# Where two roots, one sum of squares and the first sums stand in a fused two-block kernel

## What is computed

```
h = rmsnorm(x, norm_mix[l])                       # first layer: x / sqrt(mean(x*x) + eps) * gain
proj = einsum('btd,de->bte', h, w_in[l])
...
y = ssd_chunked(xh, dt, a, bm, cm) + d_skip[:, None] * xh
y = y.reshape(bsz, seq, D_SSD) * silu(z)
yg = y.reshape(bsz, seq, SSD_GROUPS, D_SSD // SSD_GROUPS)        # two halves of 512 channels
yg = yg * rsqrt(mean(yg * yg, axis=-1, keepdims=True) + EPS)     # a root for each half
y_ssd = yg.reshape(bsz, seq, D_SSD) * norm_w
...
q = rms_norm(q, q_norm_w); k = rms_norm(k, k_norm_w)             # norms by head, next stage
```

## Time and profile before

| what | us |
|---|---|
| median of 3 runs (lowest, highest) | 2328.26 (2328.11, 2329.42) |
| the profiled execution | 2329.49 |
| its span, first to last instruction | 2327.3 |
| PE busy in it | 2270.1 (98%) |
| VectorE busy | 1140.6 (49%) |
| ScalarE busy | 980.1 (42%) |
| GpSimd busy | 980.8 (42%) |
| mean granted clock of PE | 0.993 |

### The profile page before, as it was taken

One profiled execution on the slowest core, in us unless ns is written; L12 is line 12 of the kernel. 1 busy time (PEld: TensorE's weight loads), 2 busy tenths in 40 slices (PEclk: granted clock), 3 DMA queues, 4 the chain that ended last, 5 costly groups with the idle time before them and its releaser, 6 DMA issues.

```text
span 2327.3 us, 29177 instructions
## 1 busy us (share of the span) xinstructions
PE 2270.1 (98%) x10536; PEld 1791.7 (77%) x10560; DVE 1140.6 (49%) x1475; ACT 980.1 (42%) x1489; POOL 980.8 (42%) x453
## 2 busy tenths in 40 slices
PE   7989999999999999999999999999999999999999
PEld 6866678888888876678888887876777667888887
DVE  6866664222334786665222334647776543433300
ACT  5546643222214545644333213335535663534311
POOL 5962234444443982234444443432442113544442
PEclk9999999999999999999999999999999999999999
DMA  4321123333662221123323472322121002332332
GB/s 161 91 63 56 55 82 91 95 95 99 199 210 79 89 75 46 55 73 91 99 90 99 161 240 87 91 82 63 57 86 50 28 28 72 109 93 96 99 93 88
DMA packets 59842, 216.00 MB, mean 93 GB/s; under 512 B 6640, under 2 KB 6896, under 8 KB 59760
## 3 DMA queue, kind: packets, MB, share of 16 engines
q1 hardware_dynamic: 52272, 187.62, 26.4%
q10 hardware_dynamic: 7488, 27.27, 3.5%
HBM read 212.76 MB, written 2.10 MB: 92 GB/s over the span
## 4 chain that ended last, share of the span: by engine, by line
PE 88%; DVE 6%; ACT 3%; issue 2%; DMA 0%; SPq 0%; DVEq 0%; ACTq 0%
PE bank L1305 26%; PE bank L1307 26%; PE bank L1306 26%; PE bank L1770 1%; PE bank L1448 1%; PE bank L1318 1%; PE bank L1774 1%; PE bank L1508 1%; PE bank L1488 1%; PE bank L1379 1%; PE bank L1758 1%; PE bank L1374 1%; ACT prob L497 1%; DVE tmp L1233 1%; DVE tmp L1227 1%
## 5 line engine op out<-in xcount | busy, mean ns | idle before, releaser
L310 POOL TENSOR_TENSOR wl<-raw,wh 128x1024 fp32r<-128x1024 f32 x351 | 855.0, 2437 | 1301.9 <-ACT wh L383 1301.9
L1305 PE MATMUL bank<-hh,wh 128*128 128x512 f32 x2024 | 815.9, 403 | 28.4 <-DMA cst<-consts 11.7
L1307 PE MATMUL bank<-hh,wl 128*128 128x512 f32 x2024 | 793.1, 392 | 0.0
L1306 PE MATMUL bank<-hl,wh 128*128 128x512 f32 x2024 | 792.7, 392 | 0.0
L383 ACT ACTIVATE wh<-raw 128x1024 fp32r<-128x1024 f32 x351 | 369.6, 1053 | 631.8 <-PE bank L1307 580.7
L1305 PEld LDWEIGHTS bank<-hh,wh 128*128 128x128 f32 x2024 | 383.3, 189 | 122.5 <-issue 18.9
L1306 PEld LDWEIGHTS bank<-hl,wh 128*128 128x128 f32 x2024 | 383.4, 189 | 86.6 <-issue 9.6
L1307 PEld LDWEIGHTS bank<-hh,wl 128*128 128x128 f32 x2024 | 382.5, 189 | 81.7
L1305 PE MATMUL bank<-ah,wh 128*128 (+1 forms) x528 | 208.1, 394 | 0.0
L1307 PE MATMUL bank<-ah,wl 128*128 (+1 forms) x528 | 207.0, 392 | 0.0
L1306 PE MATMUL bank<-al,wh 128*128 (+1 forms) x528 | 204.9, 388 | 0.0
(11 more groups left out here) (325 smaller groups left out, 2555.7 us busy)
## 6 DMA issues: line engine op xcount, KB each, us to landing
raw<-stream SPq DMA_DIRECT2D x351, 512.0 KB, 3.6
ada_w<-ada ACTq DMA_DIRECT2D x48, 512.0 KB, 4.6
x<-x_t ACTq DMA_DIRECT2D x4, 512.0 KB, 7.9
out_t<-x SPq DMA_DIRECT2D x8, 256.0 KB, 2.1
cst<-consts SPq DMA_DIRECT2D x1, 640.0 KB, 4.8
tmp<-masks SPq DMA_DIRECT2D x1, 320.0 KB, 5.1
par<-params SPq DMA_DIRECT2D x1, 253.0 KB, 6.1
cst<-consts SPq DMA_DIRECT2D x1, 224.0 KB, 9.6
```

Of the source, the lines that this page charges most:

```text
L310: nc.gpsimd.tensor_tensor(wl[:, slot, :], raw[:, raw_slot, :], wh[:, slot, :].bitcast(F32), ALU.subtract).then_inc(lo_ready, 1)
L1305: mm(dst, wh[:, slot, w], xh, start=start, stop=False)
L1306: mm(dst, wh[:, slot, w], xl, start=False, stop=False)
L1307: return mm(dst, wl[:, slot, w], xh, start=False, stop=stop)
```

## The change

It moves work and adds none.

- ScalarE, pair loop: the root of the first half goes from turn 5 to behind the last turn, directly ahead of the second half's root. The copy of v tile 5, which stood ahead of that root, is again taken in turn 6 like the others.
- VectorE: the first half's reciprocal and its four products go from turns 5, 6 and 7 to behind the loop; there each half now has a reciprocal and four products, one half behind the other.
- ScalarE, q tiles: the eight copies of normed y go from ahead of the q tiles to behind the rounding of a chunk in the first of them, ahead of that tile's square.
- PE, q tiles: the last sum of squares of y and the last turn of v go from ahead of kk 6 of q tile 0 to ahead of kk 0 of q tile 1.
- PE, start of the first layer: the wait for the constants goes from ahead of the first matmul to ahead of `sum_both_ways`, and that goes from behind the two first tiles to ahead of kk 7 of the first tile. The second layer keeps its order.

```
@@ scalar, pair loop
             for t in range(1, KT):
                 exp_within(t)
-                if t != 6:
-                    copy_v(t - 1)
+                copy_v(t - 1)
...
                 square(SB + S_SSD + t - 1, z[:, t - 1, :])
-                if t == 5:
-                    copy_v(5)
-                    root_of(SB + S_SSD + 4, bank[:, 4, :], bank[:, 4, :], 1.0 / (D // 2))
             copy_v(KT - 1)
...
             put_v(KT - 1)
+            root_of(SB + S_SSD + 4, bank[:, 4, :], bank[:, 4, :], 1.0 / (D // 2))
             root_of(SB + S_SSD + 8, bank[:, 5, :], bank[:, 5, :], 1.0 / (D // 2))
-            for t in range(KT):
-                act.wait_ge(y_normed, t + 1)
-                af(sh_[:, t, :], z[:, t, :], ACT.Copy).then_inc(ssdh_ready, 1)
...
                 round_chunk(CB + B_Q + i + RW)
+                for t in range(KT if i == 0 else 0):
+                    act.wait_ge(y_normed, t + 1)
+                    af(sh_[:, t, :], z[:, t, :], ACT.Copy).then_inc(ssdh_ready, 1)
@@ vector, pair loop and behind it
-                if t == 5:
-                    invert(bank[:, 4, :], bank[:, 4, :])
-                if t >= 6:
-                    normed_y(2 * t - 12)
-                    normed_y(2 * t - 11)
             finish_y(KT - 1)
-            invert(bank[:, 5, :], bank[:, 5, :])
-            for t in range(4, KT):
-                normed_y(t)
+            for h in range(2):
+                invert(bank[:, 4 + h, :], bank[:, 4 + h, :])
+                for t in range(4 * h, 4 * h + 4):
+                    normed_y(t)
@@ tensor, start and q tiles
-            pe.wait_ge(consts_in, 16)
...
                             with_inputs(kk)
+                        if s == 0 and kk == KT - 1:
+                            pe.wait_ge(consts_in, 16)
+                            sum_both_ways(SQ_MIX + KT - 1)
...
-                sum_both_ways(s0 + SQ_MIX + KT - 1)
+                if l:
+                    sum_both_ways(s0 + SQ_MIX + KT - 1)
...
-                    if i == 0 and kk == 6:
+                    if i == 1 and kk == 0:
                         sum_y(KT - 1)
                         turn_v(KT - 1)
```

## The result

The changed kernel takes 2335.32 us (median of 14 runs, 2332.35 to 2341.50) where the kernel before takes 2328.31 in the same rounds (14 runs, 2326.63 to 2331.78): 7.0 us more, a ratio of 1.003 with an interval of 1.0021 to 1.0038. That is slower by more than the 0.2% that a measurement of this kernel can tell. Predicted were 2335.5, or +7.2. The profiled execution is one of the longer ones, 2338.87 us with a span of 2336.8, so 9.5 more than the span before; where the 2.5 us by which this exceeds the 7.0 of the medians come from is part of what follows.

What follows compares the result with a forecast made beforehand. The matrix engine (PE) was taken to bound the kernel. Start -0.3, tail +5.6 (loop's 1.72 inside) and clock +1.9 gave +7.2 us: 2336.7 for the profiled execution, 2335.5 as median, range 2332.6 to 2338.2.

Steps and rivals of the forecast that it cites:

- The tail: First q tiles: the serial chain with a second reciprocal and four products delays the first sum of head squares, +5.6 us.
- The loop: Loop over head pairs: the turn with the first root becomes like its neighbours, 1.72 us off PE's path.
- The clock: Behind PE's 8.2 us gap ahead of the q tiles' head squares: slow stretch at 0.50, +1.9 us, bounds 0 and 2.7.
- The start: First tile: PE starts 2.0 us sooner, but little is kept; -0.3 us, bounds -0.3 and +0.8.
- rival (c): Start: gap at 12 to 13.8 leaves PE slow until 18.9; +0.8 for -0.3, in all +8.3 us; chance 0.12.
- The sum: Whole kernel: -0.3 + 5.6 + 1.9 = +7.2 us.
- (b): Behind the tail's gap: the clock costs nothing noticeable, only the gap's length counts; +5.3 us, 2333.6; chance 0.08.
- (a): Batching ScalarE's roots wins and nothing of the tail shows; -2.0 us, 2326.2; chance 0.07.
- (d): Tail: GpSimd's remainders hold up VectorE's products; +10 us, 2338.5, if two were held; chance 0.08.

Runs made afterwards that it cites:

- t_rest: The changed kernel with the start of the kernel before, so loop and tail alone; 2340.46 us, ratio 1.0050 to the kernel before; repeated, 2335.20 us.
- t_one_recip: t_rest with VectorE's reciprocal of the first half over 16 of its 512 columns only; 2332.34 us, ratio 1.0016 to the kernel before.
- t_sum_early: t_rest with the last sum of squares and turn of v back in q tile 0 ahead of kk 6; 2335.72 us, ratio 1.0028.
- t_filled: t_rest with 34 added matmuls that nobody reads, put where PE would wait; 2332.84 us, ratio 1.0021 to the kernel before.
- s_start: The kernel before with only the changed start; 2331.63 us, ratio 1.0008 to the kernel before.
- b_best: t_sum_early with the first half's root in the last loop turn behind the exponentials, its reciprocal following there; 2325.28 us, ratio 0.9983 to the kernel before.
- b_best_start: b_best with the changed start on top; 2325.09 us, ratio 0.9989 to the kernel before.

## Why the prediction was right

**The tail (+5.6, with the loop's 1.72 inside).** Right in every link. PE's wait was to be 8.2 us and is 8.10, in the changed kernel, in t_rest and in both repetitions. The first sum of head squares moved by 7.3 us against the end of the loop, and 5.6 + 1.72 is 7.3. The second reciprocal with its four products was put at 6.15; in the trace it is from 1670.67 to about 1676.8. t_one_recip showed that the reciprocal is on the path for its whole length, t_sum_early that the later start of the chain is, for 1.36 us where I had worked with 1.38, and t_filled that the length alone costs 5.25 us in its trace (5.3 ±1.1 in time x clock).

**The loop (-1.72).** Right: 1.73, and the turns are all at 9.9. What I did not count is the 0.2 us of the turns behind it.

**The clock (+1.9).** The mechanism was right, and the term was somewhat small: behind the wait PE worked slowly for 4.3 to 5.9 us in four executions, which costs 2.0 to 2.8, and 2.7, the upper of my bounds, in the profiled one. The nearest rows I had were weak ground. The 4 us of 1961.5 to 1965.5 were where I had ended my reading and not where the stretch ended (1965.8), and the 5 us at 1445 stood behind 1.71 us of idle time and 48 matmuls of one column, not behind a gap half as long as this one. That t_filled shows 1.00 throughout and loses no clock on the mean, with the same chain, makes the gap the cause of the stretch.

**The start (-0.3).** In the profiled execution it was rival (c): PE slow until 19, the sums at 24.62 where I allowed 24.5 for that case, the third tile 1.0 later where I had +0.8 as the bound. In s_start's execution PE did what I forecast, with the sums at 23.79 behind 1.11 us of wait, and even there the third tile began 0.24 later than before. Two steps failed. Which of the two courses PE takes is not fixed; it changes with the execution. And the -0.3 was too good even for the better course: it rests on VectorE's last addition at 22.68, the earliest of 13 profiled executions (the others have 22.69 to 23.29), and on sums that start at once behind it, where they start 0.15 later. Over all runs the start is near zero (+0.4 ±0.5 in time x clock), and +0.8 lies nearer to the traces than -0.3.

**The sum.** +7.2 predicted, +7.0 measured. With a start of 0, 2.7 for the clock and the 0.2 of the last turn the same sum gives +8.1. That too lies in the measured interval (1.0021 to 1.0038 is +4.9 to +8.8), so the closeness of the two numbers is partly luck. The sharper test is the stretch from turn 4 to the long wait: 5.6 + 1.9 = 7.5 predicted, 7.28 to 8.03 in four traces. The range of 2332.6 to 2338.2 is a little wider than its own terms: (b) less half a microsecond is 2333.1, and the upper bounds of clock and start with half a microsecond give 2337.9.

**The rivals.** (a), *batching wins*, falls with the 8.10 us, and b_best says what was missing in it: its -2.0 is reached and passed by a kernel in which ScalarE batches and VectorE does not (-2.7 and -2.9, with the 0.8 of the tail beside the 1.7 of the loop). The Trainium skill's rule (ScalarE: Activation LUTs, section Table sets: the hidden batching unit) holds for the engine that it is about, since two roots behind one load take less of ScalarE here; taken for a rule about the kernel's time it led to 0.3% more, because it moves what hangs on the first root as well. (b), *only the length*, falls with the stretch at 0.50 and with the difference that filling makes. (d), *VectorE held up*, falls (the 2.29 us that I gave there for one product beside GpSimd is the row of two; a single one of 2.30 stands at 17.60 in the same timeline): the eight products take 2.72 us for four, in both halves, although GpSimd makes its remainders of y from 1669.52 on. Each reads one operand from PSUM, as I had argued from the earlier trace rows.

**What stays open.** Behind the wait of 1.2 us at the start PE is at full speed at once in s_start and b_best_start and not in the other three. In those two the trace notes the rise of the clock at 13.3, inside the wait, and in the others only at 17.8 to 19.0. Why it rises so early in some executions, and what makes the stretches near 153, 866 or 1959 longer or shorter, is not shown by any run here. Nor was it tried to fill the wait at the start.

## What to carry to other kernels

Batching a function on one engine also batches what hangs on its results on the next one: ask of the second engine how long its work is and whether anything lies between it and the bounding engine's next wait. Batch the roots but not what follows them, if the first result can be taken as soon as the last function of the other kind is through. And where a wait on the bounding matrix engine grows to some microseconds, price it with a slow stretch behind it, about half of that stretch on top of the wait: here 2.0 to 2.8 us behind 8.1 us of wait.

## What the hardware showed that I had not expected

In a kernel whose PE is busy 97 to 98% of the time, most of the scatter between runs goes with the granted clock: the mean clock runs from 0.989 to 0.995, and in the table above 0.003 of it is 6 us, nearly as much as the whole change. Comparing time x clock made a difference of 2.5 us readable with ten runs. One trace of each kernel was sharper still: the time between two landmarks around the change, with the other slow stretches left outside, agrees within 0.02 us among the three kernels that are the same there, and within 0.01 among the three versions of b_best.

How long the matmuls at the start are slow is not a property of the kernel. The Trainium skill says so too (TensorE: Matmul & The Clock Gate, section Part 1: The HAM clock gate): the same kernel shows different counts from run to run. The two profiled starts of the changed kernel agree: full speed from 19.1 in one and from 17.9 in the other.

Matmuls that nobody reads keep the clock: 34 of them in a wait of 8 us held it at 1.00 and took 2.0 to 2.8 us off between the landmarks, and 2.4 off the median of the same kernel without them, measured in other rounds. As long as the chain behind the wait can't be shortened, this is the cheap half of the remedy; the other half, as b_best shows, is not to have the wait.
